# Eight-head attention: value products of two query tiles side by side, with the values stationary and the probabilities normalised before the turn

## The chip, the cores and the metric

The kernel runs on one core of one Trainium2 chip. Times are device microseconds (us) of one execution. The time of the kernel before is 2274.74 us, the median of 3 runs (2273.14, 2274.74 and 2276.80 us).

## What is computed

The reference is two transformer blocks over 512 positions of width 1024 (the second with 16 meta tokens ahead). The change touches only the front part of the first block, whose two attentions share one input. Cut to what matters:

```python
# latent attention: 8 heads, query and key 64 + 32 wide, value 64 wide, causal
sc = (q_nope . k_nope + q_rope . k_rope) * 96 ** -0.5      # per head: 512 x 512
p = softmax(where(causal, sc, -inf))
o_b = einsum('bhqs,bshd->bqhd', p, v)                      # per head: 512 x 64
# indexed attention: 8 query heads on 2 key heads, 64 wide, each query on its 128 best keys
iscore = sum_h wi[h] * relu(qi[h] . ki);  idx = top_k(iscore, 128)
o_a = softmax(q . k[idx] / 8) . v[idx]
merged = sigmoid(g_a) * (o_a @ w_branch_a) + sigmoid(g_b) * (o_b @ w_branch_b)
```

In the kernel the latent attention is "B1" and the indexed one "A1".

## The kernel before

All work of the front part is one list, `FRONT_ORDER`, written by `work_of_front`. Every engine walks the same list and does its own part of each entry, in order; semaphores join them. No engine can pass over an entry that waits.

The **dense** work is a sequence of projections ("items"). An item is up to 8 tiles of 128x128 weights, and each tile is three products with 512 columns (split weights and inputs: high*high, low*high, high*low; L1220). Even and odd items use two slots: two banks of PSUM and two buffers `raw`, `w_hi`, `w_lo`. For an item, a DMA brings `raw`, ScalarE (ACT) rounds it to `w_hi` (`split_hi`, L1710) and VectorE (DVE) makes the rest `w_lo` (`split_lo`, L2272). The split for item j+2 can start once item j is done, and stands in the list at the next attention entry behind it (`split_item(later)`, in ACT's and DVE's walks alike). PE waits for it with `split0` or `split1` ahead of the item's first tile. ACT also takes each finished item out of PSUM (`take_item`).

Between the dense tiles stands the attention, in units v. Units 0 to 31 are the 8 heads of B1, four query tiles of 128 each (v = 4*head + tile); units 32 to 63 are A1, two heads at a time. `slot(v)` lists the entries around unit v. For B1 they are:

- `score`: PE multiplies 128 queries by 512 keys (L1250); DVE adds the causal mask, scales, copies to SBUF and finds the row maximum (L2354 to L2360); ACT takes the exponential with its row sum (`exps`, L1781), placed behind a later turn.
- `turn`: PE transposes the four 128x128 blocks of a unit's probabilities (L1286), ACT copies them to `pt` (L1790), and DVE inverts the row sum (`invert`, L2369).
- `value`: PE multiplies with the turned probabilities stationary and 64 columns of values moving (L1296); ACT scales the 128x64 result by the inverse row sum into `front_rows` (`take_output`, L1801).
- `oturn`: once per two heads, PE transposes the four blocks of `front_rows` (L1329), ACT writes the rounded 128x512 result `hid_hi` (L1817) and DVE the rest `hid_lo` (`take_low`, L2376).
- `vturn`: PE transposes a head's values (L1319) and ACT copies them (L1808).
- `rope`: rotary step of a projected query or key (PE L1237, DVE L2340 and L2344, GpSimd L1115).
- `top`: one round of finding the 128 best keys for A1, 64 rounds in all, three for each two units of B1: DVE `MAX8` and `MATCH_REPLACE8` (L2259, L2260). Behind every sixteenth round stand two more DVE operations on the mask and ahead of the next another (L2262, L2263, L2257).

During a head k of 0 to 5, the dense items are the next heads' key and value projection `bkv` (1 tile), its query projection `bq` (2 tiles) and its gate (8 tiles), 11 tiles in all. During heads 6 and 7 they are three items of 8 tiles each.

The A1 units are already done the other way round (`values_of_pair`, L1309): values stationary (64 columns), the turned probabilities of two heads moving (128 columns), the two heads in the upper and lower half of the same PSUM columns, so that the result is already transposed. There the probabilities are normalised by GpSimd (L1123) ahead of the turn.

## Time and profile before

| | |
|---|---|
| median of 3 runs | 2274.74 us |
| profiled execution, its span on the page | 2277.5 us |
| PE busy, share of the span | 2219.2 us, 97% |
| DVE busy | 1243.9 us, 55% |
| ACT busy | 903.5 us, 40% |
| GpSimd busy | 220.5 us, 10% |
| longest idle of ACT in this part: `aux` L1801 waiting for PE L1296 | 47.3 us, 23 times |

The page gives no time for the profiled execution besides its span; the span is 2.8 us over the median and 0.7 us over the slowest of the three runs. The B1 units run from about 130 to 300 us, A1's from there to about 425 us. Shares are averages over the whole span: what one engine has to spare in this stretch is read from windows of it.

### The profile page before, as it was taken

To read this page: it belongs to the slowest core of one execution; us is meant where nothing else is said; L and a number is where in the kernel's file an instruction comes from. 1 tells how busy PE (TensorE), PEld (TensorE's weight loads), DVE (VectorE), ACT (ScalarE), POOL (GpSimd) and SP (SyncE) were. 2 spreads that over 40 slices of the span, in tenths; PEclk is the share of its full clock that TensorE was granted. 3 is DMA by queue.
4 is the path that set the end of the run, shared out by engine and by line. 5 is a ranking of instruction groups with operands and counts; after the bars stand their busy time and mean duration, and the time that the engine had idled before them with its cause. 6 is when DMAs were issued, how large, how long until landed. Compare 5 with 4: busy or idle time off the path is not lost.

```text
span 2277.5 us, 36049 instructions
## 1 busy us (share of the span) xinstructions
PE 2219.2 (97%) x12592; PEld 1820.2 (80%) x12592; DVE 1243.9 (55%) x2668; ACT 903.5 (40%) x1815; POOL 220.5 (10%) x201
## 2 busy tenths in 40 slices
PE   8999999999999999999999899999999999999998
PEld 6567766778888889999999777777777787888887
DVE  5779786467736745533442545544555655443442
ACT  5455445444414443322322444444444433322332
POOL 0100043310000031000001000111100130000001
PEclk9999999999999999999999999999999999999999
DMA  4111211235533342342233222243333233332332
GB/s 119 36 37 37 65 47 52 79 102 150 157 102 95 113 129 78 91 129 88 85 106 99 57 85 81 74 111 94 98 92 98 81 97 89 95 108 77 97 105 75
DMA packets 400393, 205.67 MB, mean 90 GB/s; under 512 B 68956, under 2 KB 393928, under 8 KB 400284
## 3 DMA queue, kind: packets, MB, share of 16 engines
q1 hardware_dynamic: 399365, 203.83, 31.3%
q8 instruction: 63, 1.03, 0.2%
q10 hardware_dynamic: 919, 0.43, 0.1%
q14 instruction: 46, 0.38, 0.1%
HBM read 201.94 MB, written 14.80 MB: 95 GB/s over the span
## 4 chain that ended last, share of the span: by engine, by line
PE 64%; issue 19%; DVE 4%; ACT 2%; POOL 1%; POOLq 0%; DVEq 0%; ACTq 0%
PE acc L1169 34%; PE acc L1474 16%; PE acc L1220 5%; PE sco L1509 2%; PE acc L1573 1%; PE acc L1569 1%; DVE w_lo L2272 1%; PE sco L1262 1%; PE sco L1549 1%; POOL vT L1095 1%; PE acc L1309 1%; PE acc L1549 0%; PE sco L1529 0%; PE acc L1296 0%; DVE bias L2260 0%
## 5 line engine op out<-in xcount | busy, mean ns | idle before, releaser
L1710 ACT ACTIVATE w_hi<-raw 128x512 fp32r<-128x512 f32 (+4 forms) x656 | 372.0, 614 | 694.4 <-PE acc L1169 661.2
L2272 DVE TENSOR_TENSOR w_lo<-raw,w_hi 128x512 fp32r<-128x512 f32 (+4 forms) x656 | 423.2, 685 | 143.8 <-ACT w_hi L1710 139.5
L1169 PE MATMUL acc<-xn_hi,w_hi 128*128 128x512 f32 (+1 forms) x1408 | 421.1, 340 | 2.1 <-DVE qbuf L2826 2.1
L1169 PE MATMUL acc<-xn_lo,w_hi 128*128 128x512 f32 (+1 forms) x1408 | 422.1, 340 | 0.0
L1169 PE MATMUL acc<-xn_hi,w_lo 128*128 128x512 f32 (+1 forms) x1408 | 420.3, 339 | 0.0
L1169 PEld LDWEIGHTS acc<-xn_hi,w_hi 128*128 128x128 f32 x1408 | 241.9, 188 | 35.8 <-DVE qbuf L2826 3.0
L1169 PEld LDWEIGHTS acc<-xn_lo,w_hi 128*128 128x128 f32 x1408 | 241.2, 188 | 31.2 <-issue 0.5
L1169 PEld LDWEIGHTS acc<-xn_hi,w_lo 128*128 128x128 f32 x1408 | 241.5, 188 | 30.0
L1169 PE MATMUL acc<-hid_lo,w_hi 128*128 128x512 f32 (+1 forms) x832 | 261.5, 349 | 0.0
L1169 PE MATMUL acc<-hid_hi,w_lo 128*128 128x512 f32 (+1 forms) x832 | 260.6, 348 | 0.0
L1169 PE MATMUL acc<-hid_hi,w_hi 128*128 128x512 f32 (+1 forms) x832 | 259.8, 347 | 0.8 <-DVE hid_lo L2768 0.8
L2826 DVE TENSOR_TENSOR qbuf<-acc,v_tok 128x512 f32<-128x512 f32 (+1 forms) x132 | 91.7, 695 | 249.8 <-PE acc L1169 249.7
L1474 PE MATMUL acc<-xn_hi,w_hi 128*128 128x264 f32 (+1 forms) x576 | 187.7, 367 | 13.2 <-DVE xn_lo L2299 3.8
L2778 DVE SCALAR_TENSOR_TENSOR h<-acc,h 128x512 f32 (+3 forms) x64 | 44.5, 695 | 267.6 <-PE acc L1169 267.6
L1474 PE MATMUL acc<-xn_hi,w_lo 128*128 128x264 f32 (+1 forms) x576 | 172.8, 341 | 0.0
L1474 PE MATMUL acc<-xn_lo,w_hi 128*128 128x264 f32 (+1 forms) x576 | 172.5, 340 | 0.0
L1169 PEld LDWEIGHTS acc<-hid_hi,w_hi 128*128 128x128 f32 x832 | 144.5, 188 | 23.2 <-issue 1.1
L1169 PEld LDWEIGHTS acc<-hid_lo,w_hi 128*128 128x128 f32 x832 | 144.5, 188 | 21.2
L1169 PEld LDWEIGHTS acc<-hid_hi,w_lo 128*128 128x128 f32 x832 | 144.8, 188 | 20.4
L1474 PEld LDWEIGHTS acc<-xn_hi,w_hi 128*128 128x128 f32 x576 | 98.7, 189 | 36.8 <-issue 17.8
L1220 PE MATMUL acc<-xn_hi,w_hi 128*128 128x512 f32 x240 | 118.6, 494 | 0.9 <-DVE w_lo L2272 0.6
L1474 PEld LDWEIGHTS acc<-xn_hi,w_lo 128*128 128x128 f32 x576 | 99.3, 189 | 12.6
(397 smaller groups left out, 3065.7 us busy)
## 6 DMA issues: line engine op xcount, KB each, us to landing
raw<-in_w_ffn_in SPq DMA_DIRECT2D x176, 256.0 KB, 3.0
raw<-in_w_in SPq DMA_DIRECT2D x118, 256.0 KB, 3.2
raw<-in_w_up SPq DMA_DIRECT2D x88, 256.0 KB, 3.0
raw<-in_w_ffn_out SPq DMA_DIRECT2D x32, 384.0 KB, 3.3
raw<-in_w_gate SPq DMA_DIRECT2D x48, 256.0 KB, 3.0
raw<-in_w_ffn_out SPq DMA_DIRECT2D x32, 320.0 KB, 3.7
...
```

What stands on the lines that cost most here:

```text
L1095: ins = pool.tensor_tensor(square_sum[:, c0:T], square_sum[:, c0:T], probs[:, s, c0:T], ALU.add)
L1169: mm = pe.matmul(acc[0:m, 2 * slot + b, 0:size], w[slot][:, t, 0:m], x[:, place(t), c:c + size], start=(t == 0 and w is w_hi and x is xh), ...
L1220: mm = pe.matmul(acc[0:m, slot, 0:SEQ], w[slot][:, t, 0:m], x[:, t, META:T], start=(t == 0 and w is w_hi and x is xh), stop=(t == tiles - ...
L1262: mm = pe.matmul(sco[:, hh, :], queries_a[i][r, P * (t - 1):P * t], kbuf[r, i // 2, META:T], start=True, stop=True)
L1309: mm = pe.matmul(acc[64 * hh:64 * hh + 64, 3, o:o + P], front_values(u)[:, 1 + b, 0:64], pt[:, hh, 1 + b, :], start=b == 0, stop=b == 3)
L1474: mm = pe.matmul(acc[:, b if wide else slot, 0:size], w[slot][:, t, :], x[:, t, c:c + size], start=(t == 0 and w is w_hi and x is xh), sto ...
L1509: mm = pe.matmul(sco[:, bank, to:to + size], qbuf[r, i % 2, TILES[t][0]:TILES[t][0] + P], kbuf[r, keys_at(name, i), c:c + size], start=Tru ...
L1549: mm = pe.transpose(turned_of[x % 2][:, b * P:(b + 1) * P], prob_of[u % 4][:, real + b * P:real + (b + 1) * P], eye)
L1710: act.activation(w_hi[slot][:, a:b, :], raw[slot][:, a:b, :], ACT.Copy).then_inc(S[f"hi_ready{slot}"], parts)
L2272: dve.tensor_tensor(w_lo[slot][:, a:b, :], raw[slot][:, a:b, :], w_hi[slot][:, a:b, :].bitcast(F32), ALU.subtract).then_inc(S[f"split{slot ...
L2778: dve.scalar_tensor_tensor(out=x, in0=banks(acc, 2 * s, blk), scalar=factor, in1=x, op0=ALU.mult, op1=ALU.add).then_inc(S[f"acc_free{s}"], 1)
L2826: dve.tensor_tensor(span(scaled[s], blk), banks(acc, 2 * s, blk), span(rstd, blk), ALU.mult).then_inc(S[f"acc_free{s}"], 1)
```

## The change

Units 0 to 31 are done like A1's, but two query tiles of one head stand side by side in place of two heads, and ACT normalises in place of GpSimd. The entries `value` and `oturn` are gone; `tiles` w stands for units 2w and 2w+1.

- PE: `values_of_tiles` (L1293 of the changed kernel) runs 8 products per pair, values stationary (64 columns), 128 columns of probabilities moving, where `values` ran 4 per unit with 64 columns moving. The 16 transposes of `turn_outputs` are gone. `turn_probs` waits for the unit's normalised probabilities (`tile_normal`) in place of its exponentials (`probs`).
- ACT: `normalize_tile(u)` (L1782) is new: 128x512, in place, scaled by the inverse row sum, one per unit, behind `take_probs(u - 1)`. `take_tiles` (L1790) rounds two 64x128 results; `take_output` and `take_outputs` are gone.
- DVE: `take_tiles` (L2360) makes two 64x128 rests per pair in place of a 128x512 one per 8 units; `invert(j + 1)` stands at turn j, one entry of that kind earlier than before.
- Order: in `slot(v)`, `tiles` stands ahead of the turn of an odd v, and the turns, scores and dense tiles move accordingly. GpSimd's and the DMA queue's work stays as it was.

```diff
-        if v + 1 < FRONT_VALUES:
-            e += [("turn", v + 1), None]
+        if v % 2:
+            e += [("tiles", v // 2), None]
+        e += [("turn", v + 1), None]
         if v + 4 < 32:
             e += [("score", v + 4), None]
...
-        e += [("value", v), None]
-        if v % 8 == 7:
-            e += [("oturn", v // 8), None]
+        if v % 2 == 0:
+            e.append(None)
         rounds = range(3 * v // 2, 3 * (v + 1) // 2)
...
+        def front_tiles(w, hh):
+
+            head, t, _ = front_unit(2 * w + hh)
+            at, o, d = META + P * (t - 1), P * (w % 2), 64 * (head % 2)
+            return [x[d:d + 64, head // 2, at:at + P] for x in outputs["B1"]], acc[64 * hh:64 * hh + 64, 3, o:o + P]
...
                     if v < 32:
-                        pe.wait_ge(S["probs"], n.at("probs", v + 1))
+                        pe.wait_ge(S["tile_normal"], n.at("tile_normal", v + 1))
...
-                def values(v):
...
-                    for b in range(4):
-                        mm = pe.matmul(acc[:, 3, 64 * (v % 2):64 * (v % 2) + 64], pt[:, v % 2, 1 + b, :],
-                                       front_values(v)[:, 1 + b, 0:64], start=b == 0, stop=b == 3)
+                def values_of_tiles(w):
...
+                    for b in range(4):
+                        for hh in range(2):
+                            mm = pe.matmul(acc[64 * hh:64 * hh + 64, 3, o:o + P], front_values(u)[:, 1 + b, 0:64],
+                                           pt[:, hh, 1 + b, :], start=b == 0, stop=b == 3)
...
+                def normalize_tile(u):
+
+                    act.wait_ge(S["rinv"], n.at("rinv", u + 1))
+                    act.activation(front_probs[u % 4], front_probs[u % 4], ACT.Copy,
+                                   scale=rinv8[:, u % 8:u % 8 + 1]).then_inc(S["tile_normal"], 1)
+
+                def take_tiles(w):
+
+                    act.wait_ge(S["o_full"], n.at("o_full", w + 1))
+                    for hh in range(2):
+                        (hi, _), bank = front_tiles(w, hh)
+                        last = act.activation(hi, bank, ACT.Copy)
+                    last.then_inc(S["o_hi"], 1)
...
                     elif what == "turn":
+                        if j == 0:
+                            normalize_tile(0)
                         take_probs(j)
+                        if j + 1 < 32:
+                            normalize_tile(j + 1)
                         for u in asked:
                             exps(u)
...
-                        if j < 32:
-                            invert(j)
+                        if j == 0:
+                            invert(0)
+                        if j + 1 < 32:
+                            invert(j + 1)
```

How this moves the instructions, at the three places that matter below.

PE, at the start of head 0: from the score behind unit 1's turn on, before. The item in slot 0 is `bkv` (1 tile), the one in slot 1 `bq` (2 tiles, 96 columns of weights).

```order
L1250 MATMUL sco<-kbuf,qbuf 128x512 [waits scored,acc_free0,roped]
L1220 MATMUL acc<-hid_hi,w_hi0 128x512 [waits acc_free0,split0]
L1220 MATMUL acc<-hid_lo,w_hi0 128x512
L1220 MATMUL acc<-hid_hi,w_lo0 128x512
L1296 MATMUL acc<-v_tok,pt 128x64 [waits o_out,pt_a]
L1296 MATMUL acc<-v_tok,pt 128x64 x3
L1220 MATMUL acc<-hid_hi,w_hi1 96x512 [waits acc_free1,split1]
L1220 MATMUL acc<-hid_lo,w_hi1 96x512
L1220 MATMUL acc<-hid_hi,w_lo1 96x512
L1286 MATMUL acc<-const,aux 128x128 [waits pt_a,probs]
```

The same place of the changed kernel.

```order
L1247 MATMUL sco<-kbuf,qbuf 128x512 [waits scored,acc_free0,roped]
L1217 MATMUL acc<-hid_hi,w_hi0 128x512 [waits acc_free0,split0]
L1217 MATMUL acc<-hid_lo,w_hi0 128x512
L1217 MATMUL acc<-hid_hi,w_lo0 128x512
L1217 MATMUL acc<-hid_hi,w_hi1 96x512 [waits acc_free1,split1]
L1217 MATMUL acc<-hid_lo,w_hi1 96x512
L1217 MATMUL acc<-hid_hi,w_lo1 96x512
L1293 MATMUL acc<-pt,v_tok 64x128 [waits o_out,pt_a]
L1293 MATMUL acc<-pt,v_tok 64x128 x7
L1217 MATMUL acc<-hid_hi,w_hi1 96x512
```

The value products stood ahead of the first `bq` tile; now the first `bq` tile, which waits for its split, stands ahead of them. The first gate tile, which waits for the gate's split, comes two dense tiles, a score and a turn behind the value products before, and one dense tile and a turn behind them now.

ACT, in head 1, from taking the `bkv` item on, before (the slot with 128x512 is the gate's split, the one with 128x128 the next `bkv`'s).

```order
L1755 ACTIVATE kbuf<-acc 64x512 [waits item_done0]
L1756 ACTIVATE vT<-acc 64x512
L1801 ACTIVATE aux<-acc,stats 128x64 [waits pt_full,rinv,o_full]
L1710 ACTIVATE w_hi0<-raw0 128x512 [waits item_done0,raw_in0]
L1710 ACTIVATE w_hi0<-raw0 128x512
L1790 ACTIVATE pt<-sco 128x512 [waits o_full,pt_full]
L1781 ACTIVATE probs,stats<-probs,stats 128x512 [waits rinv,negm]
L1751 ACTIVATE qbuf<-acc 96x512 [waits item_done1]
L1801 ACTIVATE aux<-acc,stats 128x64 [waits rinv,o_full]
L1710 ACTIVATE w_hi1<-raw1 128x128 [waits item_done1,raw_in1]
```

The changed kernel, a head later.

```order
L1741 ACTIVATE kbuf<-acc 64x512 [waits item_done0]
L1742 ACTIVATE vT<-acc 64x512
L1790 ACTIVATE hid_hi<-acc 64x128 [waits o_full]
L1790 ACTIVATE hid_hi<-acc 64x128
L1696 ACTIVATE w_hi0<-raw0 128x512 [waits item_done0,raw_in0]
L1696 ACTIVATE w_hi0<-raw0 128x512
L1737 ACTIVATE qbuf<-acc 96x512 [waits item_done1]
L1776 ACTIVATE pt<-acc 128x512 [waits o_full,pt_full]
L1782 ACTIVATE aux<-aux,stats 128x512 [waits rinv]
L1767 ACTIVATE probs,stats<-probs,stats 128x512 [waits rinv,negm]
L1696 ACTIVATE w_hi1<-raw1 128x128 [waits item_done1,raw_in1]
```

The next `bkv`'s split stands behind the same turn's copy, a normalisation and an exponential, and no longer behind a value product of its own.

DVE, in head 2, from the gate's split on, before.

```order
L2272 TENSOR_TENSOR w_lo0<-raw0,w_hi0 128x512 [waits hi_ready0] x2
L2259 MAX small<-bias 128x8
L2260 MATCH_REPLACE bias<-small,bias 128x512 [waits top_step]
L2369 RECIPROCAL stats<-stats 128x1 [waits o_out,probs,top_step]
L2354 COPY small<-small 1x1 [waits pt_full,s_full]
L2355 ISA probs,stats<-sco,bias 128x512
L2355 ISA stats 128x1
L2360 TENSOR_SCALAR stats<-stats 128x1 [waits scored]
L2340 TENSOR_TENSOR qbuf<-sco,aux 96x512 [waits cos_done,turned]
L2344 TENSOR_TENSOR qbuf<-qbuf,bias 96x512 [waits rope_step]
L2272 TENSOR_TENSOR w_lo1<-raw1,w_hi1 128x128 [waits hi_ready1]
```

The same place of the changed kernel.

```order
L2243 MAX small<-bias 128x8
L2244 MATCH_REPLACE bias<-small,bias 128x512 [waits top_step]
L2360 TENSOR_TENSOR hid_lo<-acc,hid_hi 64x128 [waits o_hi,top_step]
L2360 TENSOR_TENSOR hid_lo<-acc,hid_hi 64x128
L2256 TENSOR_TENSOR w_lo0<-raw0,w_hi0 128x512 [waits hi_ready0] x2
L2353 RECIPROCAL stats<-stats 128x1 [waits tile_normal,probs]
L2256 TENSOR_TENSOR w_lo1<-raw1,w_hi1 128x128 [waits hi_ready1]
L2324 TENSOR_TENSOR qbuf<-sco,aux 96x512 [waits cos_done,turned]
L2328 TENSOR_TENSOR qbuf<-qbuf,bias 96x512 [waits rope_step]
L2338 COPY small<-small 1x1 [waits pt_full,s_full]
```

The round and the score that stood between the two splits are now on either side of them: the split of the next `bkv` follows the gate's with one reciprocal between, and the rotary step and the score stand behind both.

## Rows read from the trace of the kernel before

**Rows 1.** Windows, heads 0-5, 1, 5, 6-7: length, PE, PEld, DVE, ACT, GpSimd busy, clock

```profile
131.59:244.81 113.22, 110.13 (x584) 80.78 (x583) 97.67 (x274) 64.34 (x154) 7.66 (x6) 1.00 0.18 45
150.57:169.12 18.55, 18.48 (x101) 13.60 (x100) 14.56 (x42) 10.88 (x26) 1.29 (x1) 1.00 0.14 38
225.40:244.81 19.41, 18.71 (x101) 13.54 (x100) 17.07 (x47) 11.62 (x27) 1.28 (x1) 1.00 0.34 82
244.81:301.24 56.43, 56.02 (x280) 42.11 (x279) 41.90 (x103) 26.37 (x60) 9.55 (x7) 1.00 0.19 47
```

**Rows 2.** Chain that ended last, head 6: start us, us, what

```profile
266.73 0.44 PE sco L1286 x4
...
269.44 1.39 PE acc L1220 x6
270.82 0.84 PE acc L1296 x8
271.66 1.45 PE acc L1220 x6
```

**Rows 3.** The same chain in the A1 units

```profile
331.91 1.02 PE acc L1309 x16
332.93 0.89 PE acc L1220 x3
```

**Rows 4.** Timeline of DVE, head 1, unit 5: start us, us

```profile
158.99 0.69 DVE L2340 TENSOR_TENSOR qbuf<-sco,aux 96x512 f32<-96x512 f32 x1
...
160.32 0.28 DVE L2272 TENSOR_TENSOR w_lo<-raw,w_hi 128x128 fp32r<-128x128 f32 x1
160.52 0.68 DVE L2259 MAX8 small<-bias 128x8 f32<-128x512 f32 x1
...
163.55 0.17 DVE L2369 RECIPROCAL stats<-stats 128x1 f32<-128x1 f32 x1
...
164.51 0.68 DVE L2259 MAX8 small<-bias 128x8 f32<-128x512 f32 x1
```

**Rows 5.** Timeline of ACT, head 0

```profile
135.08 0.58 ACT L1755 ACTIVATE kbuf<-acc 64x512 f32<-64x512 f32 x1
...
136.29 0.31 ACT L1801 ACTIVATE aux<-acc,stats 128x64 f32<-128x64 f32 x1
136.50 1.14 ACT L1710 ACTIVATE w_hi<-raw 128x512 fp32r<-128x512 f32 x2
137.54 0.58 ACT L1790 ACTIVATE pt<-acc 128x512 f32<-128x512 f32 x1
138.02 0.72 ACT L1781 ACTIVATE probs<-probs,stats 128x512 f32<-128x512 f32 x1
...
138.73 0.58 ACT L1751 ACTIVATE qbuf<-acc 96x512 f32<-96x512 f32 x1
...
141.55 0.30 ACT L1710 ACTIVATE w_hi<-raw 128x128 fp32r<-128x128 f32 x1
```

**Rows 6.** Timeline of the A1 units: a pair's products and what takes them

```profile
339.37 1.09 PE L1309 MATMUL acc<-pt,v_tok 128*64 128x128 f32 x16
...
340.51 0.28 ACT L1823 ACTIVATE hid_hi<-acc 128x128 fp32r<-128x128 f32 x1 [3.12 <-PE acc L1309]
...
341.24 0.29 DVE L2382 TENSOR_TENSOR hid_lo<-acc,hid_hi 128x128 fp32r<-128x128 f32 x1
```

**Rows 7.** Timeline of PE, head 3: first tile of the query item

```profile
191.59 0.48 PE L1220 MATMUL acc<-hid_hi,w_hi 128*96 128x512 f32 x1 [0.23 <-DVE w_lo L2272]
```

**Rows 8.** Timeline of DVE and PE, head 5: turn 24 and the mask

```profile
237.89 0.43 DVE L2262 TENSOR_SCALAR bias<-bias 128x512 f32<-128x512 f32 x1
...
238.45 0.60 PE L1286 MATMUL sco<-const,probs 128*128 128x128 f32 x4
...
239.86 0.69 DVE L2259 MAX8 small<-bias 128x8 f32<-128x512 f32 x1
...
241.38 0.16 DVE L2369 RECIPROCAL stats<-stats 128x1 f32<-128x1 f32 x1
```

87 lines of the change are left out of this document (28 added, 59 removed).

## The prediction

> **What bounds the kernel now.** I read the page first: TensorE (PE) is busy for nearly all of the span, so the thought behind the change is natural, namely that fewer PE instructions are less time. But the change lies in 170 us only, so the next view is windows over that stretch, cut where a head's values are transposed. In heads 0 to 5 a head takes 113.22 / 6 = 18.87 us, PE is busy for 97% of it and VectorE (DVE) for 86%: 97.67 of 113.22 us [rows 1]. In head 5 DVE is busy for 17.07 of 19.41 us. In heads 6 and 7 (28.2 us each) DVE is busy for 74% and PE for 99%. So PE bounds heads 6 and 7, and in heads 0 to 5 it bounds by a margin of some 2 us per head, which DVE has free. Then the chain of waits and the timelines, for the cost of each piece.
>
> **PE's side of the change.** Before: the four products of a unit take 0.84 us in the chain and the six dense products behind them 1.45 in place of 1.39 us [rows 2], so a unit costs 0.90 us. After: the same form of instruction runs in the A1 units, 16 records for 8 products, 1.02 us per pair, and the three dense products behind them take 0.89 us, where three others take 1.39 / 2 = 0.70 [rows 2, 3]; so a pair costs 1.02 + 0.19 = 1.21 us. The 32 units cost 28.8 us and will cost 16 x 1.21 = 19.4: PE is relieved of 9.4 us. The 16 transposes of four `oturn` entries cost 4 x 0.44 [rows 2] = 1.8 us. Together 11.2 us, 1.16 us per head and 1.8 besides.
>
> Side by side does not mean at the same time here: 16 records in 1.02 us are 64 ns each, one behind the other [rows 3]. The Trainium skill (TensorE: Matmul & The Clock Gate, Part 3) says that products in different column groups of the array run concurrently, starting some 4 ns apart; the pair would then cost about half, and PE would be relieved of some 8 us more. The row is of this very form, so the sum keeps 1.02.
>
> **What the other engines get.** ScalarE (ACT), per unit: a 128x512 normalisation. Its nearest rows are the copy to `pt`, behind which the next instruction starts after 0.48 us, and the exponential, after 0.71 [rows 5]; I take 0.60, and keep both ends. Per pair two 64x128 roundings; a 128x128 one lasts 0.28 us [rows 6] and overlaps the next by 0.1, so 0.36 for both. It loses 32 scalings of 0.21 (136.29 to 136.50) and four 128x512 copies. ACT's sum grows by some 2.5 us per head, and it was busy for 64.34 of 113.22 [rows 1]: its sum is covered, its place in the order is not (below). DVE, per pair, two rests of 0.2 (0.29 long, overlapping [rows 6]): 0.40, against four 128x512 ones of 0.6 in all: 12 x 0.40 - 3 x 0.6 = +3 us over six heads. DVE's own sum would be about 100.7 of 113.2 us, so by sums PE could still gain it all. GpSimd and the DMA queues do the same as before; transfers have their slack.
>
> **The order, and the cycle it closes.** Three moves matter. (1) The first `bq` tile stands ahead of the products now. It waits for DVE's split, which stands behind two rounds of `top`; already before, PE waited there by 0.23 us [rows 7], with a unit's products (0.84 us) to bridge. (2) The gate's split stands behind the pair's products on ACT and DVE, and PE wants it one dense tile and a turn later (0.70 + 0.44 us), where it had 2.7 us. (3) The next `bkv`'s split is made by ACT behind a turn's copy, a normalisation and an exponential, and DVE waits for it ahead of rope, score and rounds, in order. So once per head, from the start of DVE's `bq` split:
>
> - DVE's split and reciprocal 0.50; ACT then normalises 0.60, takes the exponential 0.71 and the `bkv` item 1.21 (135.08 to 136.29 [rows 5]): it comes to the pair's result at 3.05. PE's way there is shorter: split about 0.43 (between 0.28 for 128 columns [rows 4] and the double of it), tile 0.80, products 1.09 [rows 6]: 2.4.
> - ACT: roundings 0.36, gate's split 1.04, `bq` item 0.49, turn's copy 0.48, normalisation 0.60, exponential 0.71, `bkv` split 0.30 [rows 5]: 3.98.
> - DVE: `bkv` split 0.20, rope 1.33, score 0.88, two rounds 3.03, reciprocal and score 0.96, one round 1.51, the pair's rests 0.40, reciprocal and score 0.96, two rounds 3.03 [rows 4]: 12.30. Then the next `bq` split.
>
> 3.05 + 3.98 + 12.30 = 19.3 us per head, whatever PE saves. PE's own sum is below 17.7 + waits, so it stands idle for 2 us of each: at the first `bq` tile and at the first gate tile. Before there was no such circle, since DVE could run its rounds while ACT and PE did the rest; the 2 us that DVE had free per head are spent in waiting for the `bkv` split.
>
> Heads 0 to 4: 5 x 19.3 = 96.5 us. In head 2 the sixteenth round falls, with 1.97 us more between the rounds (237.89 to 239.86 [rows 8]); it lies in the circle, with nothing to cover it: 98.5. Head 5: from the head's start to the products 4.4 us. From there turn 24 waits for its normalisation, that for the reciprocal, and that stands on DVE behind both splits (8-tile ones now), rope, score and two rounds with the mask work: 5.4 us to the end of ACT's exponential, half a split 0.57, DVE 1.21 + 1.33 + 0.88 + 3.03 + 1.97 + 0.16, normalisation 0.7 = 15.2. Before, PE did turn 24 at 238.45 while the reciprocal that now has to come first was DVE's at 241.38 [rows 8]: nothing waited for it but the scaling. Then 2.8 to the head's end: 22.4. Six heads: 98.5 + 22.4 = 120.9 against 113.2, +7.7 us. Heads 6 and 7 have 8-tile items, and PE's turns there are 7 us apart, so PE's saving goes through: 2 x 1.16 + 0.44 = 2.8. Sum: +4.9 us. Units from 32 on are as before and start later by that.
>
> The profiled execution's span is 2277.5 us, 2.8 over the median of the runs; the difference is carried to the median: 2274.74 + 4.9 = **2279.6 us**. About 0.2%, 4.5 us, is what a measurement of this kernel can tell from no change; the forecast lies at that edge.
>
> **Rivals.**
> (a) *The circle is there but shorter.* If ACT takes the `bkv` item ahead of the pair in time (2.4 for 3.05) and normalises in 0.48, a head takes 19.33 - 0.65 - 0.12 = 18.6: 3.5 us less over five heads, +1.4 us, 2276.1. For it: that all durations of the circle lean on ones that overlap. Against: the exponential behind it has 0.71.
> (b) *PE's sum goes through: faster.* If DVE and ACT keep ahead, it is -11.2 us: 2263.5; with the skill's concurrency some 2256, 1 in 100. For it: PE 97% busy, DVE's sum under the new length. Against: the in-order waits above. It decides if PE never waits at the `bq` tile; half of it, -5.6, if only every other head waits.
> (c) *A longer circle.* Normalisation at the exponential's 0.71 twice per head, and turns that come late, so that ACT's copies and with them all that stands behind move back by half a microsecond more: 20.1 per head, +9 us, 2284. The Trainium skill (TensorEngine Tiling (Array Packing), PSUM Bottleneck) says that tiling speeds up TensorE but not the copies out of PSUM, which may become the bound. It would point this way: 64x128 pieces, twice as many instructions per result; rows 6 show only the 128x128 ones.
> (d) *The change does nothing on PE*, if PE's relief is refilled exactly, in no time lost: near 2275, part of "same".
>
> **Chances.** Forecast with its bounds 0.5 (a little over half of it above 4.5 us), (a) and (d) 0.26, (b) 0.12, (c) 0.12. From these: faster 0.12, same 0.36, slower 0.52. The range goes from half of (b), 2269.5, to (c) with its own spread, 2286.
>
> **What would show it.** After: windows from one transpose of values to the next about 19.3 us in heads 1, 3, 4, 21.3 in head 2, 22.4 in head 5, 27 in 6 and 7; PE waiting 1 us or more on DVE `w_lo` at the first 96-column tile and 0.5 to 1 at the first gate tile; DVE waiting some 2 us for ACT's 128-column `w_hi` in each head; PE waiting 3 us ahead of turn 24. Pair products 1.02 us and normalisations near 0.6. I am wrong if DVE does not wait for that `w_hi`, or if heads 1 to 4 fall below 18 us.

## The result and the profile after: 2300.2 us, 1.1% slower

| | before | after |
|---|---|---|
| median | 2275.12 us (4 runs) | 2300.21 us (4 runs, 2298.21 to 2304.49) |
| ratio | | 1.0106, interval 1.0093 to 1.0118 |
| profiled execution, its span | 2277.5 us | 2299.6 us |
| PE busy, span | 2219.2 us | 2217.2 us |
| six heads, 0 to 5 | 113.22 us | 127.48 us |
| heads 6 and 7 | 56.43 us | 58.99 us |

The forecast was 2279.6 (2269.5 to 2286). The sign came as forecast, and so did the circle in heads 0 to 4; the size did not, it is five times as much. The medians are 25.1 us apart and the two profiled executions 22.1: that of the kernel before was 2.4 us above its median of four runs, that of the change 0.6 below. Windows of the changed kernel; columns as in [rows 1] (length, PE, PEld, DVE, ACT and GpSimd busy, granted clock, DMA). The rows are heads 0 to 5, head 1, head 5, heads 6 and 7, and three pieces of 5 us.

```profile
133.39:260.87 127.48, 107.38 (x571) 68.94 (x570) 103.14 (x294) 77.65 (x175) 7.68 (x6) 0.97 0.16 40
153.03:173.33 20.30, 17.38 (x97) 11.13 (x96) 16.76 (x49) 12.76 (x30) 1.28 (x1) 1.00 0.13 34
235.78:260.87 25.09, 18.96 (x96) 12.27 (x95) 19.64 (x54) 14.51 (x33) 1.29 (x1) 0.93 0.25 64
260.87:319.86 58.99, 55.48 (x275) 38.71 (x274) 39.70 (x106) 29.65 (x64) 9.48 (x7) 0.97 0.16 41
255.00:260.00 5.00, 3.54 (x10) 2.58 (x10) 3.55 (x12) 3.80 (x8) 0.00 (x0) 0.66 0.01 2
280.00:285.00 5.00, 2.74 (x18) 1.64 (x18) 2.33 (x8) 1.91 (x4) 1.26 (x1) 0.87 0.02 3
285.00:290.00 5.00, 5.00 (x23) 3.73 (x21) 3.67 (x9) 3.19 (x7) 0.00 (x0) 0.79 0.05 4
```

PE's work fell (head 1 from 18.48 us busy to 17.38), and the head became longer (18.55 to 20.30): PE stands idle for 2.92 us of it, and for 0.07 before. The waits of heads 0 to 7 (133.39 to 319.86) say for whom; engine, what it was about to do, for whom it waited, us in total, times, longest.

```profile
ACT probs L1782 <- DVE stats L2353: 34.1, 13, 6.9
DVE w_lo L2256 <- ACT w_hi L1696: 23.6, 9, 4.6
PE acc L1217 <- DVE w_lo L2256: 14.6, 11, 2.1
ACT aux L1782 <- DVE stats L2353: 12.6, 7, 2.3
DVE hid_lo L2360 <- ACT hid_hi L1790: 7.3, 8, 1.3
PE sco L1280 <- ACT probs L1782: 3.9, 3, 3.5
```

All three engines wait for each other. PE waits 14.6 us for splits (the kernel before: 0.8 us in the same eight heads). The largest pair is one that the prediction has once per head in its circle and in head 5, and at nothing in heads 6 and 7: **ACT's normalisation (L1782) waits 34.1 + 12.6 = 46.7 us for DVE's reciprocal (L2353)**. ACT works in order, so its splits and item copies wait along with it.

The circle, once around, in head 1 (timeline; start, us, what, and the idle time ahead of it; a choice of rows, others stand between them):

```profile
156.48 0.42 DVE L2256 TENSOR_TENSOR w_lo<-raw,w_hi 128x256 fp32r<-128x256 f32 x1
156.96 0.48 PE L1217 MATMUL acc<-hid_hi,w_hi 128*96 128x512 f32 x1 [1.34 <-DVE w_lo L2256]
157.01 0.72 ACT L1782 ACTIVATE aux<-aux,stats 128x512 f32<-128x512 f32 x1 [1.68 <-DVE stats L2353]
157.83 1.09 PE L1293 MATMUL acc<-pt,o_tok 128*64 128x128 f32 x16
159.55 0.55 ACT L1790 ACTIVATE hid_hi<-acc 64x128 fp32r<-64x128 f32 x2
160.13 1.15 ACT L1696 ACTIVATE w_hi<-raw 128x512 fp32r<-128x512 f32 x2
160.21 0.59 DVE L2360 TENSOR_TENSOR hid_lo<-acc,hid_hi 64x128 fp32r<-64x128 f32 x2 [1.00 <-ACT hid_hi L1790]
161.57 0.50 PE L1217 MATMUL acc<-xn_hi,w_hi 128*128 128x512 f32 x1 [1.35 <-DVE w_lo L2256]
163.99 0.29 DVE L2256 TENSOR_TENSOR w_lo<-raw,w_hi 128x128 fp32r<-128x128 f32 x1 [1.79 <-ACT w_hi L1696]
...
169.72 0.72 ACT L1782 ACTIVATE probs<-probs,stats 128x512 f32<-128x512 f32 x1 [3.70 <-DVE stats L2353]
...
176.79 0.43 DVE L2256 TENSOR_TENSOR w_lo<-raw,w_hi 128x256 fp32r<-128x256 f32 x1
```

From DVE's `bq` split at 156.48 to ACT's roundings 3.07 us, to DVE's `bkv` split 4.44, to the next `bq` split 12.80: 20.31. These are the stations of the prediction, in its order. At 157.01 ACT has waited 1.68 us for the reciprocal that DVE makes behind two rounds and that very split. At 169.72 it has waited another 3.70, which is not on the circle: PE's next turn is late by 0.24 us, and DVE does not stand idle between 163.99 and 176.79.

And head 5, timeline of ACT and PE around turn 24:

```profile
255.48 0.16 DVE L2353 RECIPROCAL stats<-stats 128x1 f32<-128x1 f32 x1
...
255.68 0.72 ACT L1782 ACTIVATE probs<-probs,stats 128x512 f32<-128x512 f32 x1 [6.92 <-DVE stats L2353]
...
256.46 1.12 PE L1280 MATMUL sco<-const,probs 128*128 128x128 f32 x4 [3.45 <-ACT probs L1782]
257.22 0.78 PE L1217 MATMUL acc<-xn_hi,w_hi 128*128 128x512 f32 x1
257.80 0.63 PE L1217 MATMUL acc<-xn_lo,w_hi 128*128 128x512 f32 x1
258.22 0.63 PE L1217 MATMUL acc<-xn_hi,w_lo 128*128 128x512 f32 x1
```

Turn 24 comes where the prediction put it, with PE idle for 3.45 us (forecast: 3). What follows it was not foreseen: dense products start 0.42 us apart and not 0.23, at a granted clock of 0.66 over 255 to 260, that is, for most of these 5 us at the lower of the two levels.

One more wait stands ahead of head 0. The first turn waits for the first normalisation, which stands on ACT behind an exponential and an item's copy (timeline of ACT and PE; in the kernel before this turn has no wait):

```profile
131.18 0.71 ACT L1782 ACTIVATE probs<-probs,stats 128x512 f32<-128x512 f32 x1
131.94 0.66 PE L1280 MATMUL sco<-const,probs 128*128 128x128 f32 x4 [1.71 <-ACT probs L1782]
```

### The profile page after: what moved, and what is told of

Read it like the earlier page. It is cut to its first block, busy times and chain, and to the rows that moved or that the text cites. A ratio compares the mean times of both kernels' runs of the same rounds, so it can differ in the third digit from the quotient of the medians.

```text
span 2299.6 us, 36031 instructions
## 1 busy us (share of the span) xinstructions
PE 2217.2 (96%) x12576; PEld 1806.5 (79%) x12576; DVE 1250.0 (54%) x2696; ACT 921.3 (40%) x1843; POOL 220.2 (10%) x201
## 4 chain that ended last, share of the span: by engine, by line
PE 80%; DVE 4%; ACT 3%; issue 2%; POOL 1%; DMA 0%; SPq 0%; DVEq 0%; ACTq 0%; POOLq 0%
PE acc L1169 52%; PE acc L1460 15%; PE acc L1217 4%; PE sco L1495 2%; PE acc L1559 1%; DVE w_lo L2256 1%; PE acc L1555 1%; PE sco L1535 1%; PE sco L1259 1%; PE acc L1306 1%; PE acc L1535 0%; DVE bias L2244 0%; PE sco L1515 0%; ACT w_hi L1696 0%; DVE small L2243 0%
## 5 line engine op out<-in xcount | busy, mean ns | idle before, releaser
L1169 PEld LDWEIGHTS acc<-hid_hi,w_hi 128*128 128x128 f32 x832 | 144.6, 188 | 23.6 <-issue 1.6
L1169 PEld LDWEIGHTS acc<-hid_lo,w_hi 128*128 128x128 f32 x832 | 144.6, 188 | 21.1
L1169 PEld LDWEIGHTS acc<-hid_hi,w_lo 128*128 128x128 f32 x832 | 145.0, 189 | 20.3
```

What stands on the lines that cost most here:

```text
L1169: mm = pe.matmul(acc[0:m, 2 * slot + b, 0:size], w[slot][:, t, 0:m], x[:, place(t), c:c + size], start=(t == 0 and w is w_hi and x is xh), ...
```

## The experiments

All times are medians; the ratio is to runs of the kernel before on the same chip (2275 to 2277 us). The length of each head is read as in the table of windows: from one transpose of values on PE to the next.

| run | median us | ratio (interval) | heads 0, 1, 2, 3, 4, 5 | 6, 7 |
|---|---|---|---|---|
| before | 2275.1 | | 18.98 18.55 18.80 18.67 18.81 19.41 | 28.24 28.19 |
| the change | 2300.2 | 1.0106 (1.0093 to 1.0118) | 19.64 20.30 20.19 22.06 20.20 25.09 | 31.08 27.91 |
| before_rounds_out | 2275.3 | 0.9990 (0.9980 to 1.0000) | 18.95 18.55 18.60 18.55 18.62 18.55 | 28.24 28.19 |
| rounds_out | 2270.1 | 0.9969 (0.9957 to 0.9980) | 19.32 17.77 17.64 17.79 17.64 18.43 | 26.95 27.94 |
| norm_out | 2279.3 | 1.0011 (1.0001 to 1.0020) | 18.03 19.27 19.18 21.68 19.21 19.27 | 26.97 27.32 |
| order_alone | 2300.5 | 1.0100 (1.0077 to 1.0123) | 19.70 24.27 23.67 24.68 20.67 24.51 | 29.43 30.41 |
| order_now | 2288.6 | 1.0049 (1.0033 to 1.0066) | 20.75 20.30 19.91 20.31 19.88 23.02 | 29.46 30.41 |
| split_now | 2306.1 | 1.0125 (1.0108 to 1.0142) | 19.89 22.26 21.49 23.64 22.89 23.45 | 31.05 27.91 |
| pool_norm | 2305.6 | 1.0126 (1.0109 to 1.0143) | 19.84 21.53 23.04 23.24 20.81 26.81 | 27.20 29.62 |
| third_buffer | 2319.5 | 1.0186 (1.0169 to 1.0203) | 23.23 24.35 25.17 23.84 22.75 29.56 | 28.06 27.98 |
| third_now | 2329.9 | 1.0224 (1.0207 to 1.0241) | 25.43 26.60 26.47 27.40 26.69 31.57 | 28.91 27.96 |
| bridged | 2304.1 | 1.0122 (1.0106 to 1.0139) | 21.28 21.12 21.13 21.81 21.16 24.75 | 32.98 27.92 |
| bridged_five | 2298.3 | 1.0102 (1.0080 to 1.0124) | 22.10 20.31 20.20 22.06 20.20 25.16 | 31.05 27.92 |
| recip_early | 2288.1 | 1.0059 (1.0042 to 1.0076) | 19.28 19.49 20.26 22.92 19.65 19.56 | 28.33 27.94 |
| recip_early_third | 2294.2 | 1.0080 (1.0063 to 1.0097) | 22.02 20.22 20.37 22.51 22.02 20.25 | 28.17 26.62 |
| recip_early_now | 2280.2 | 1.0018 (1.0008 to 1.0028) | 19.66 17.45 17.48 21.81 17.49 17.45 | 28.26 27.94 |
| spread | 2280.7 | 1.0017 (1.0007 to 1.0026) | 18.33 17.44 17.47 17.47 17.95 17.47 | 26.96 31.93 |
| before_spread | 2277.7 | 1.0004 (0.9995 to 1.0014) | 18.99 18.54 18.82 18.55 18.81 18.54 | 28.24 28.19 |
| deal_two | 2277.9 | 1.0002 (0.9993 to 1.0012) | 18.32 17.45 17.47 17.47 17.97 17.45 | 26.95 29.83 |
| deal_two_now | 2273.7 | 0.9985 (0.9976 to 0.9994) | 18.31 17.45 17.47 17.47 17.97 17.45 | 26.97 28.77 |

The shortest heads of the change's form are 17.45 us: PE is busy for 16.94 to 16.96 of them and waits once, 0.5 us, for `w_lo`. The kernel before has PE busy for 18.08 us in heads 2 and 4, and for 18.48 in head 1, where 0.44 of it are the transposes of `oturn`. So the change takes 1.10 to 1.13 us per head off PE by the form of the products (forecast: 1.16), and the 0.44 in every second head besides. The question is what makes a head longer than 17.45.

### Does the circle run through DVE's rounds?

```diff
                 here, there = (isc[j], ping) if r % 2 == 0 else (ping, isc[j])
-                top(dve.max(max8, here))
-                top(dve.match_replace(there, max8, here, TAKEN))
+                if j == 3:
+                    top(dve.max(max8, here))
+                    top(dve.match_replace(there, max8, here, TAKEN))
```

> The kernel before, with the MAX8 and MATCH_REPLACE of the top rounds of the first three key tiles left out (48 rounds, heads 0 to 7; the mask comes out another). Taken as the base for rounds_out. TensorE is busy for 97% of heads 0 to 5, so little goes: 2268 to 2274 by both theories.

> The change with the same 48 rounds left out. Theory (circle through VectorE's rounds): VectorE's part of the circle falls by 7.5 us per head, TensorE is the bound, and the change now gives what it saves on TensorE: 9 to 11 us less than before_rounds_out, near 2260. Rival (form of the products, or normalisation ahead of each transpose, is the cost): 10 us or more above before_rounds_out, 2280 or more.

Measured: 2275.3 (just above the 2268 to 2274 that were expected) and 2270.1 (expected: near 2260). With the rounds gone, the same products, normalisations and 64x128 pieces, in the same order, are 5.2 us faster than the kernel before with its rounds gone. That excludes that the form of the products or the added work as such makes the time. Of the 9 to 11 us expected about half came: heads 1 to 4 fall by 0.76 to 0.98 each and not by 1.1, head 6 by 1.3, heads 5 and 7 by 0.1 and 0.3, and head 0 is 0.4 longer.

```profile
151.28:169.05 17.77, 16.95 (x97) 11.28 (x96) 8.55 (x31) 12.94 (x29) 1.29 (x1) 1.00 0.15 40
```

That is the window of head 1 in rounds_out: DVE is busy for 8.55 us (16.76 in the change), ACT for as long as in the change (12.94), and PE has 17.77 us instead of 20.30.

### Does the normalisation lengthen it?

The call of `normalize_tile` is left out, the transpose waits for the exponential:

```diff
-                        pe.wait_ge(S["tile_normal"], n.at("tile_normal", v + 1))
+                        pe.wait_ge(S["probs"], n.at("probs", v + 1))
...
-                        if j + 1 < 32:
-                            normalize_tile(j + 1)
```

> The change with the normalisation left out (the probabilities stay unnormalised; a transpose waits for the exponential alone; the reciprocals are still made). Theory: two normalisations of 0.62 to 0.72 leave the circle, 20.3 - 1.4 = 18.9 us per head in heads 1, 3 and 4; turn 24 no longer waits for a reciprocal behind two rounds, head 5 about 20.5 for 25.1; heads 6 and 7 about 27 each, since ScalarE is not blocked there: 2300.2 - 7 - 4.5 - 5 = 2284 (2280 to 2288). Rival (side-by-side products or 64x128 pieces are the whole cost): 2297 or more, heads still above 20.

Measured: 2279.3, 21 us below the change, 5 more than expected and just outside the range. Heads 1, 2 and 4 are 19.2 (forecast 18.9), head 5 is 19.27 with no wait ahead of turn 24. The 32 normalisations are 32 x 0.61 = 20 us on an engine that is idle for 37% of head 1, and their removal gives back 21 us. That the two numbers agree is chance. Heads 1, 2 and 4 give 1.0 us each, head 5 gives 5.8, head 6 gives 4.1 and the stretch ahead of head 0 1.9: most of it are waits that the normalisations bring, not their own time. Heads of 19.2 are still 1.75 above the 17.45.

### The order alone, in the kernel before

```diff
         if v + 1 < FRONT_VALUES:
-            e += [("turn", v + 1), None]
+        if v % 2:
+            e += [("value", v - 1), ("value", v), None]
+        if v % 8 == 7:
+            e += [("oturn", v // 8), None]
+        e += [("turn", v + 1), None]
...
-        e += [("value", v), None]
-        if v % 8 == 7:
-            e += [("oturn", v // 8), None]
+        if v % 2 == 0:
+            e.append(None)
```

> The kernel before, with its own products (probabilities stationary), its scaling by ScalarE and its turning of the outputs, but walked in the order of the change: the products of units 2w and 2w+1 stand one behind the other where the pair stands now. Theory (the circle is made of the added work of ScalarE and VectorE together with the order): start of the bq split to the pair's result 2.9, roundings to the bkv split 3.4 (no normalisation, two scalings of 0.21), VectorE 11.9 (no rests): 18.2 us per head, under TensorE's own 18.7, so a head takes 18.9 to 19.2 and the time is 2275 to 2278. Rival 1 (the order alone is the cost): 2290 or more. Rival 2 (the new form of the products is the cost): 2275, and after_no_norm stays near 2298.

> order_alone (the kernel before in the order of the change), with the split that follows each bkv, bq and gate item of heads 0 to 5 made at once. There no reciprocal blocks ScalarE. Theory (the loop runs through the splits that stand behind the turn and the scalings): TensorE's own 18.6 to 19.2 us per head again, 2276 to 2283. Rival (pairing the products is bad by itself, wherever the splits stand): 2292 or more.

Both miss. Measured: 2300.5 and 2288.6, where 2275 to 2278 and 2276 to 2283 were expected. The first is what its rival 1 expected (2290 or more), the second lies between its theory and its rival (2292 or more). The order alone, without any normalisation or new form, costs as much as the whole change, though with a flaw of its own (below). Waits of PE in heads 0 to 7 of order_alone, and its window of head 1:

```profile
PE acc L1298 <- ACT aux L1803: 8.7, 16, 1.0
PE acc L1222 <- DVE w_lo L2274: 6.9, 5, 2.0
PE sco L1331 <- ACT aux L1803: 2.0, 1, 2.0
```
```profile
150.08:174.35 24.27, 22.05 (x101) 15.99 (x100) 16.13 (x46) 11.12 (x26) 1.29 (x1) 0.86 0.11 29
```

The first row is a flaw of the experiment: the second product of a pair waits there for the scaling of the first (0.5 us each, 8.7 in all), which the change has not. The rest looks like the circle again: DVE waits 36.0 us for `w_hi` in these heads, the kernel before 17.1. PE is busy for 22.05 us of that head for work that took 18.48 [rows 1], at a granted clock of 0.86. My sum for this circle (18.2 us) had PE's pieces at their full-clock length, and added ACT's and DVE's pieces as if each were free to start. In this kernel the scaling puts PE's products between two steps of ACT, so a slower PE can lengthen the loop; how much of the 24 us that is stays open. order_now has the granted clock at 0.99 and heads near 20. Without the 13.3 us that PE waits for scalings in its heads 0 to 7 it would be near 2275, if all of them fell away (worked out, not run). So it speaks for the splits and does not settle it alone.

### Where the reciprocal stands

Four attempts to shorten the circle were made first, without touching the reciprocal.

split_now: behind each `bkv`, `bq` and `gate` item an entry that makes both engines split at once.

```diff
+        if e[0] == "dense":
+            kind, name, index, tiles = items[e[1]]
+            if kind in ('bkv', 'bq', 'gate') and name == "B1" and index >= 2 and e[3] == tiles:
+                ahead.append(("now", e[1]))
```

> The change, with the split that follows each bkv, bq and gate item of heads 0 to 5 made at once, ahead of the pair's roundings and of the turn's copy, normalisation and exponential, on ScalarE and VectorE; nothing else moved. Theory: the bkv split stands 0.58 + 0.62 + 0.71 = 1.8 us earlier in the circle (0.48 + 0.62 + 0.71), the gate's split no longer waits for the pair: 20.3 - 1.8 = 18.5 us, TensorE's own 17.4 plus small waits; heads 0 to 4 about 9 us less in all, heads 5 to 7 as they are: 2291 (2288 to 2294). Rival (the sum of ScalarE's or VectorE's work sets the head, not its order): 2298 or more.

pool_norm: GpSimd normalises, with the instruction of the A1 units.

```diff
+                        elif what == "turn" and j < 31:
+                            for u in ((0, 1) if j == 0 else (j + 1,)):
+                                pool.wait_ge(S["rinv"], n.at("rinv", u + 1))
+                                pool.tensor_scalar(front_probs[u % 4], front_probs[u % 4], rinv8[:, u % 8:u % 8 + 1], None,
+                                                   ALU.mult).then_inc(S["tile_normal"], 1)
```

> The change, with the normalisation of units 0 to 31 made by GpSimd as the A1 units have it (1.6 us each). Theory: the circle loses two normalisations of 0.62 on ScalarE and the waits for reciprocals that block ScalarE: 20.3 - 1.2 = 19.1 us per head in heads 1, 3, 4; turn 24 still waits, for a normalisation 0.9 us longer, head 5 about 25; heads 6 and 7 about 28 each; 2300 - 5 - 3 = 2292 (2288 to 2296). Rival (each transpose now comes 0.9 us later and that is what counts): 2300 to 2310.

third_buffer: the turned probabilities go round three buffers, so that a pair's products may stand behind the next turn and score, where single products stood before.

```diff
+            if v < 32 and v % 3 == 2:
+                return aux[:, 6 * SEQ:7 * SEQ].rearrange("p (j q) -> p j q", j=4)
...
+        if v % 2 and v < 31:
+            e.append(("tiles", v // 2))
```

> The change, with a third buffer for turned probabilities (the freed 128x512 of the old outputs), so that the pair's products stand behind the next transpose and score, as the single products did before, and the first bq tile and gate tile are further from their splits. Theory: the pair is no longer between the bq split and ScalarE's way to the bkv split; that is then item bq, copy, normalisation, exponential, split: 3.05 us shorter at the head of the circle less some 0.5: about 18.3 to 18.8 us per head, 2288 to 2292 with heads 5 to 7 as they are. Rival (sum of the work): 2298 or more.

> Third buffer and splits at once together, normalisation on ScalarE. Theory: no circle is left in heads 0 to 4, TensorE's own 17.4 to 17.9 us per head; turn 24's wait for its reciprocal and heads 6 and 7 as in the change: 2300 - 5 x 2.5 = 2287 (2283 to 2291). Rival: as third_buffer or split_now alone, no sum.

All four miss, and on the wrong side: 2306.1, 2305.6, 2319.5 and 2329.9, where 2287 to 2292 were expected (2283 to 2296 with the ranges). So the splits' place was not what mattered first. The waits of ACT in heads 1 to 5 of split_now, and of third_buffer, show what did:

```profile
ACT aux L1789 <- DVE stats L2360: 22.1, 10, 3.6
ACT probs L1789 <- DVE stats L2360: 15.7, 8, 5.1
```
```profile
ACT probs L1791 <- DVE stats L2362: 18.4, 9, 5.1
ACT aux L1791 <- DVE stats L2362: 12.1, 5, 3.2
```

In five heads ACT waits 37.8 and 30.5 us for reciprocals. A reciprocal takes DVE 0.16 us, but it stands at the head of a slot, behind the rounds of the slot before, and what is moved ahead of it (the splits) makes it later still. In pool_norm it is GpSimd that waits for it, 60 us in heads 1 to 4, and the transposes wait for GpSimd. Its normalisation also takes 1.56 us for 0.72, and its rival (each transpose comes later for that, 2300 to 2310) came out; the run does not tell the two apart. So the next step was to move the reciprocal by itself:

```diff
                     elif what == "score":
                         score(j)
+                        if j >= 4:
+                            invert(j - 1)
```

(with the call at `turn` taken out but for units 0 to 2 and 31). It is made one slot earlier, ahead of that slot's rounds, and its exponential has been asked for by then.

> The change, with VectorE's reciprocal of unit v+3 made right behind the score of unit v+4, ahead of the rounds of the slot, where the change makes it behind them, at the head of the next slot; nothing else moved. In the change ScalarE waited 46.7 us for these reciprocals in heads 0 to 7, each time with its splits and item copies queued behind. Theory (reciprocal behind the rounds, ScalarE blocked by it): head 5 falls from 25.1 to about 20.5 since turn 24 comes in time, heads 6 and 7 from 59 to about 54.5, heads 1 to 4 by 0.5 each: 2300 - 4.5 - 4.5 - 2 = 2289 (2285 to 2293). Rival (these waits are slack of ScalarE and cost nothing): 2297 or more.

> recip_early with the splits at once (as split_now). Theory: split_now lost 6 us against the change because the splits it moved ahead put the next reciprocal further back; with the reciprocal ahead of the rounds that loss turns into the gain expected of it: 1 to 1.5 us per head below recip_early in heads 0 to 4, 2280 to 2285. Rival: as recip_early or above.

> recip_early with the third buffer, so TensorE's order is that of the kernel before but for the form and number of the products. Theory: third_buffer was slow (heads 24) because ScalarE stood 2 to 3 us at each normalisation for a reciprocal behind two rounds with the gate's split queued behind it, and TensorE waited 1.3 and 2.8 us for w_lo; without that wait the order of the kernel before works again: heads 18 to 18.8, heads 6 and 7 54.5 together, 2268 to 2276. Rival (order with the pair late is bad in itself, or the added work of ScalarE and VectorE in sum): 2290 or more.

Measured: 2288.1 for an expected 2289, 2280.2 for an expected 2280 to 2285, and 2294.2 for an expected 2268 to 2276. Moving 29 instructions of 0.16 us gives back 12 us of 25. That the first number hit is in part luck: heads 0 to 7 became 9.0 us shorter, 8.3 of it in heads 5 and 6. Heads 1 to 4 gave 0.4 us together, where 2 were expected, and head 5 gave 5.5 for 4.5. ACT's waits for reciprocals fall from 46.7 us to 9.4:

```profile
ACT probs L1782 <- DVE stats L2353: 9.4, 8, 2.5
```

Against the same kernels without it the reciprocal's place is worth 12 us in the change, 26 with the splits at once (2306.1 to 2280.2), and 25 with the third buffer. The splits at once, which cost 6 us in the change, bring 8 here. In heads 1 to 4 neither move works alone (82.8 us for these four in the change, 90.3 with the splits, 82.3 with the reciprocal), and both together do (74.2). Windows of recip_early_now, head 1 and head 3:

```profile
153.40:170.85 17.45, 16.94 (x96) 11.28 (x96) 16.15 (x48) 12.69 (x29) 1.31 (x1) 1.00 0.16 41
188.33:210.14 21.81, 18.70 (x96) 11.89 (x95) 19.89 (x55) 12.70 (x29) 1.27 (x1) 0.92 0.13 33
```

In head 1 PE waits once, 0.5 us, and DVE is busy for 16.15 us. The gain on PE is there, with every instruction of the change, in four heads of six. Around the start of head 3 one key tile's rounds end and the next tile's begin, with the mask's instructions between them; DVE is busy for 19.89 us there, and PE is idle for 3.11 us ahead of the gate's first tile. (The expectation of spread calls this head 2; in the change it is head 3 too, 22.06 us, where the prediction had head 2.)

recip_early_third failed. PE still waits for `w_lo` there (16.4 us in heads 1 to 5, ten times), twice per head: with the pair late, ACT splits the gate's weights behind a turn, and the `bq` split stands behind two rounds as before. It was not tried with splits at once; what it would give is open.

### Is it the half clock?

```diff
+                    if first == 0 and name == "B1" and kind in ("bq", "gate") and at >= 2:
+                        pe.wait_ge(S[f"acc_free{slot}"], n.at(f"acc_free{slot}", k - 1))
+                        for _ in range(10):
+                            pe.matmul(acc[:, slot, 0:P], ones[:, :], eye, start=True, stop=True)
```

> The change, with ten 128x128 products of ones into the accumulator that the item is about to fill, ahead of the first tile of each bq and gate item of heads 0 to 5, where TensorE stood idle for 1 to 1.4 us: it waits less and does some 1 us of work that is thrown away. Theory (half clock behind the waits lengthens TensorE's part of the circle): granted clock 1.00 in heads 0 to 4, heads 1 and 2 shorter by 0.3 to 0.8: 2295 to 2299. Rival (the clock plays no part in heads 1 to 4, where it was 1.00 already, and the filling adds its time): 2300 to 2308.

Measured: 2304.1, with heads of 21.1 us. But the experiment was mis-sized: the ten products are 20 records and take 2.16 us, where 1.35 were to be filled (timeline of PE, head 1).

```profile
154.17 2.39 PE L1202 MATMUL acc<-const,ones 128*128 128x128 f32 x20
156.32 0.47 PE L1221 MATMUL acc<-hid_hi,w_hi 128*96 128x512 f32 x1
```

With them PE is busy for the whole length of heads 1 and 2 (21.12 of 21.12 us): that run shows the filling and not the clock. So again with `range(5)`:

> As bridged with five products in place of ten, 1.08 us at each place, where TensorE waited 1.34 and 1.35 us in the change. Nothing on the circle is lengthened by it, since TensorE still waits at the end of the filling. If the clock plays a part in heads 0 to 4, these are shorter by up to 0.9 us each, 2296 to 2298; if it plays none there, heads 1, 2 and 4 stay at 20.2 to 20.3 and only head 0 (granted clock 0.91 in the change) gains some tenths: 2298 to 2301. If they become longer by 0.5 or more, the filling does harm in another way.

Measured: 2298.3, and heads 1 to 4 of 20.31, 20.20, 22.06 and 20.20 us, where the change has 20.30, 20.19, 22.06 and 20.20. Two more us of work for PE in each of these heads change nothing, to a hundredth: **PE is not on the circle in heads 1 to 4**, the loop is closed between ACT and DVE, and these heads had the full clock anyway. Head 0 went the other way: 22.10 us for 19.64, where some tenths less were expected. PE has no wait left there (22.10 us busy, granted clock 0.86), so in head 0 the filling is added to the time, and how much of that the clock makes is open.

A lower clock matters only where PE is late by it: head 0 (granted clock 0.91), the end of head 5 and head 6. As a bound, PE is busy for 107.38 + 55.48 = 162.9 us in heads 0 to 7 of the change and for 102.05 + 53.68 = 155.7 in deal_two_now below, which had 1.00 throughout, for the same products: at most some 7 of the 25 us, 5.3 of them in heads 0, 5 and 6.

### Can the gain be had?

Rounds dealt out anew, 48 as before: 5 in each of heads 0 to 5, and 9 and 9 (spread) or 11 and 7 (deal_two) in heads 6 and 7. This is deal_two's; it has unit 31's reciprocal behind pair 0's scores as well, and deal_two_now has the splits at once in heads 6 and 7 too.

```diff
-        rounds = range(3 * v // 2, 3 * (v + 1) // 2)
+        per = ((0, 1, 2, 3, 5),) * 6 + ((0, 3, 6, 9, 11), (0, 2, 4, 6, 7))
+        first = sum(x[4] for x in per[:v // 4])
+        rounds = range(first + per[v // 4][v % 4], first + per[v // 4][v % 4 + 1])
```

> recip_early_now, with the rounds dealt out another way: 5 in each of heads 0 to 5 (was 6) and 9 in heads 6 and 7 (was 6), 48 in all as before. Theory (VectorE's rounds and the mask work ahead of the gate's split make head 2's 21.8 us): heads 1 to 5 17.5 us, head 2 at most 19, head 0 about 19, heads 6 and 7 27.5 to 28.5: 2280 less 3 to 6, 2275 (2272 to 2278). Rival (something else in head 2): 2279 or more.

> The kernel before with the same dealing of the rounds. TensorE bounds it by its own work: heads of 18.55, head 5 18.6 for 19.4, the rest as it is: 2274 to 2276 by both theories. If it falls as far as spread does, the gain of spread is not the change's.

> As spread, but 11 rounds in head 6 and 7 in head 7 (spread had 9 and 9), and the reciprocal of unit 31 behind the scores of pair 0 instead of at turn 30. Theory (VectorE's rounds ahead of the ropes and of pair 1 made head 7 of spread 31.9 us): head 7 27.5 to 28.5, head 6 27 to 28, what follows as in the kernel before: 2272 to 2277, at or below the kernel before. Rival (the gain is always given back behind head 6): 2279 or more.

> deal_two with the splits behind the six items of heads 6 and 7 made at once too. Theory: these items have 8 tiles, TensorE reaches each split late, so the place of the splits matters little: within 2 us of deal_two. Rival (ScalarE blocked in heads 6 and 7 is what costs): 3 us or more below deal_two.

Measured: 2280.7, 2277.7, 2277.9, 2273.7; the first three lie above their ranges (2272 to 2278, 2274 to 2276, 2272 to 2277). spread has that head at 17.47, as the theory wants, and loses the gain in head 7 (31.93 us), which nobody had forecast: there the pair's scores wait 2.7 us for a rotary step that stands behind rounds. deal_two takes 2.1 us of that off, deal_two_now takes 1.1 more, and it is 4.2 us below deal_two, which its rival expected (3 or more) and the theory did not. The profiles show only 1.1 of these 4.2 in heads 0 to 7 (162.91 to 161.86 us). Six of deal_two's twelve runs lie at 2279 to 2280 and six at 2272 to 2277, and what sets the two groups apart is open.

before_spread shows that spread's dealing is worth nothing to the kernel before. The kernel before with deal_two's dealing and the splits at once was not run. PE is busy there for 166.15 of 169.65 us in heads 0 to 7 [rows 1], so it could gain 3.5 us in them at most. Windows of deal_two_now, heads 0 to 5 and heads 6 and 7:

```profile
134.13:240.25 106.12, 102.05 (x572) 67.59 (x571) 92.43 (x271) 77.17 (x175) 8.31 (x6) 1.00 0.19 48
240.25:295.99 55.74, 53.68 (x276) 37.51 (x275) 51.68 (x130) 29.45 (x64) 10.22 (x7) 1.00 0.21 53
```

Heads 0 to 7 take 161.86 us, 7.8 less than the 169.65 of the kernel before [rows 1]; of that 3.1 us arrive in the median, by a ratio of 0.9985 (0.9976 to 0.9994). In the two profiled executions heads 0 to 7 begin 2.5 us later there, and what follows them takes 1.7 us more. 1.9 of the 2.5 are the change's too. Between the first transposes of values and those of head 0 the kernel before takes 13.17 us and deal_two_now 15.11, with the 1.72 us wait for the first normalisation; norm_out and order_alone, which have none, take 13.21 and 13.19. What scatters is the first of these marks, 115.5 to 119.4 us over all runs. Of the 1.7 us behind head 7, 1.1 are in the stretch to the last pair of A1 (110.60 us for 109.55; before_spread, without the change, has 111.09). It is the one version that beats both kernels, by little.

## Why the prediction was wrong, point by point

By size, what failed: heads 6 and 7 (5.4 us), the terms of the circle in heads 0 to 4 (3.9), what follows head 7 (3.5), head 5 (2.7) and the start (1.8).

**PE's side held**, as a sum. The pair's products are 1.09 us long as in the A1 units [rows 6], and PE's busy time falls by 1.10 to 1.13 us per head (forecast 1.16) and by `oturn`'s 0.44 in every second. The reading "16 records in 1.02 us are 64 ns each, one behind the other" is wrong: it takes a mean for a distance. Windows of L1293 alone on PE in the change; behind the x stands the number of records begun by then.

```profile
157.82:157.83 0.01, 0.00 (x1) 1.00 0.00 0
157.83:157.84 0.01, 0.01 (x2) 1.00 0.00 0
157.97:157.98 0.01, 0.01 (x2) 1.00 0.21 51
157.98:157.99 0.01, 0.01 (x3) 1.00 0.30 77
157.99:158.00 0.01, 0.01 (x4) 1.00 0.30 77
```

The records start in twos, 7 ns apart, and the twos 0.11 us apart (0.16 between the first and the second). The products of the kernel before, with 128 columns of weights, start one by one, 0.11 us apart. The Trainium skill (TensorE: Matmul & The Clock Gate, Part 3) has products in different column groups run side by side in time, and the trace agrees as far as it goes: it does not say which products the two records of a pair belong to. This is already in the 1.02 us, so the sum stands, and the further 8 us at the end of rival (b) would have counted it twice.

**The circle was right in its stations and 1.0 us short.** It came out as 3.07 + 4.44 + 12.80 = 20.31 for a forecast of 3.05 + 3.98 + 12.30 (the pieces of the first term add up to 3.02). In the middle term the roundings took 0.58 for 0.36, the gate's split 1.17 for 1.04, the `bkv` split 0.40 to DVE for 0.30. In the last the rests took 0.63 for 0.40, the `bkv` split 0.32 for 0.20, the second reciprocal and score 1.10 for 0.96. The first step that failed is "a 128x128 one lasts 0.28 us and overlaps the next by 0.1, so 0.36 for both", with the same for the rests: two 64x128 pieces take 0.55 on ACT and 0.59 on DVE. It makes 0.45 of the 1.0 us. The Trainium skill (TensorEngine Tiling (Array Packing), PSUM Bottleneck), which warns of the copies behind tiled products, pointed the right way, and stood only in rival (c). Over heads 0 to 4 the circle's terms make 3.9 us (102.39 for 98.5). The mask work was put into head 2; it is the end of head 2 on DVE, and head 3 that is longer for it, by 1.9 us for the 2.0 of the sum.

**Normalisation** was sized rightly: 0.61 from one start to the next, for 0.60.

**Head 5**, 25.09 for 22.4. PE's wait ahead of turn 24 came as forecast (3.45 for 3), 1.1 us later. Then the head's end took 4.4 us for 2.8, at the lower clock [rows 8 are the same place before].

**Heads 6 and 7**, 58.99 for 53.6: the sentence "PE's turns there are 7 us apart, so PE's saving goes through" failed. ACT's normalisation waits for its reciprocal, and the next item copy, on which PE's rotary product depends, waits in ACT's order behind it (timeline of head 6):

```profile
280.64 0.72 ACT L1782 ACTIVATE probs<-probs,stats 128x512 f32<-128x512 f32 x1 [4.71 <-DVE stats L2353]
...
281.98 0.57 ACT L1739 ACTIVATE qbuf<-acc 128x512 f32<-128x512 f32 x1
...
282.60 1.13 PE L1234 MATMUL sco<-qbuf,const 128*128 128x512 f32 x2 [2.26 <-ACT qbuf L1739]
```

I had asked who waits for the normalisation (the turn), and not what is queued behind it. Head 6 takes 31.08 us, where norm_out and spread, without that wait, have 26.97 and 26.96: 4.1 us, of which 2.26 are the wait and the rest PE's products at the lower clock behind it. Head 7 adds another 1.2: there PE waits 1.20 us for a rotary step of DVE (L2328) ahead of the first pair's scores. rounds_out and recip_early have 1.2 there too and norm_out 0.6, so it is not the reciprocal's. Together this is the largest miss, 5.4 us.

**The start and what follows** were put at nothing. Heads 0 to 7 began 1.8 us later. The first turn's wait for its normalisation is 1.71 us of that, in every kernel here in which ACT normalises. Behind them 3.5 us more went, 2.4 of it up to the last pair of A1 (111.91 us for 109.55), where PE waits 3.7 us for 1.8 (before_spread, without the change, takes 111.09, so this is not the form of the products; it was not pursued); the rest is within what the runs scatter. Together with the above: 3.9 + 2.7 + 5.4 + 1.8 + 3.5 = 17.3, and the forecast 4.9 and the 22.1 us of the profiled executions are 17.2 apart.

**The cause behind the terms.** The prediction has the wait for the reciprocal once per head in its circle ("DVE's split and reciprocal 0.50; ACT then normalises") and at turn 24. It put it at nothing in heads 6 and 7, although it had noted that DVE makes it behind the rounds. It is the largest wait of the kernel (46.7 us), and its place alone is worth 12 us in the median (recip_early), nearly all in heads 5 and 6. For heads 1 to 4 the account is the circle's: it closes through DVE's rounds (rounds_out), the reciprocal alone or the splits alone do not open it, and both together do. DVE is not short of time there (16.15 of 17.45 us busy in recip_early_now), it is out of step.

**The signs it named.** DVE's wait for the `bkv` split (1.79 us for "some 2"), PE's wait at the first `bq` tile (1.34 for 1 or more) and ahead of turn 24 came. The wait at the gate's tile was 1.35 for 0.5 to 1, and heads 6 and 7 were 31.08 and 27.91 for 27.

**The rivals.** (a), a shorter circle, did not come: ACT reached the pair's result after 3.07 us, not 2.4. (b), PE's sum going through, is nearly what the change does once the other engines' order is made to fit (heads of 17.45). (c), 20.1 per head, was the nearest for heads 1, 2 and 4, with 0.12 of the chance and a price (+9) that left heads 5 to 7 as they were forecast. The range ended at 2286 because all of its cases took the recovery in heads 6 and 7 as certain.
